# One block's diagonal, column sums and one-hot distances: three reorderings in a single-core kernel

## The reference, cut to what matters

```python
mod = c_act @ ada_w[l] + ada_b[l]
shift1, scale1, gate1, shift2, scale2, gate2 = jnp.split(mod, 6, axis=-1)
...                                            # pooling mixer and latent attention give y
x = x + gate1[:, None, :] * rms_norm(y, post_mix_g[l])
h = modulate(rms_norm(x, pre_ffn_g[l]), shift2, scale2)
y = peer_ffn(h, peer_wq[l], peer_sub_keys[l], peer_u[l], peer_v[l])
x = x + gate2[:, None, :] * rms_norm(y, post_ffn_g[l])
```

## Time and profile before

| what | value |
|---|---|
| median of 3 runs | 2076.1 us (2073.14 to 2076.58) |
| profiled execution, its own time | 2077.25 us |
| its span, first to last instruction | 2075.3 us |
| TensorE busy | 1905.2 us, 92% |
| VectorE busy | 1492.3 us, 72% |
| ScalarE busy | 948.2 us, 46% |
| POOL busy | 658.6 us, 32% |
| mean granted TensorE clock | 0.971 |

### The profile page before, as it was taken

The page is one execution under the profiler, slowest core; times in us unless marked ns, Lnnn a source line. Parts: engine busy times, 40 slices in busy tenths (PEclk is TensorE's granted clock), DMA queues, the critical chain, the costliest instruction groups (busy, mean ns, idle before and its releaser), DMA issues.

```text
span 2075.3 us, 33816 instructions
## 1 busy us (share of the span) xinstructions
PE 1905.2 (92%) x10307; PEld 1627.5 (78%) x10307; DVE 1492.3 (72%) x2053; ACT 948.2 (46%) x1498; POOL 658.6 (32%) x347
## 2 busy tenths in 40 slices
PE   0489989899999999999999997689999999999997
PEld 0479758799788888888888886578887888788886
DVE  6998679763888889998887668967675555455555
ACT  1043344443444444445554448854444444444443
POOL 1000020000888888889974446600000000000000
PEclk9789969899999999999999999999999999999999
DMA  9989569990666666666677762057766666665554
GB/s 390 415 306 384 201 254 385 287 219 19 164 187 186 185 187 185 185 187 175 184 191 189 189 159 91 0 184 286 288 233 183 203 204 207 234 210 194 192 193 151
DMA packets 229619, 439.10 MB, mean 212 GB/s; under 512 B 23538, under 2 KB 158144, under 8 KB 216000
## 3 DMA queue, kind: packets, MB, share of 16 engines
q1 hardware_dynamic: 225648, 416.31, 63.5%
q0 software_dynamic: 3888, 22.14, 3.0%
q10 hardware_dynamic: 32, 0.01, 0.0%
HBM read 434.12 MB, written 4.21 MB: 211 GB/s over the span
## 4 chain that ended last, share of the span: by engine, by line
PE 85%; DVE 6%; issue 4%; DMA 2%; ACT 1%; POOL 1%; SPq 1%; DVEq 0%; ACTq 0%; POOLq 0%
PE ps L883 21%; PE ps L885 11%; PE ps L933 11%; PE ps L934 11%; PE ps L936 11%; PE ps L655 4%; PE ps L657 4%; PE ps L656 4%; PE ps L916 3%; DVE acc L1338 3%; PE ps L650 2%; DMA raw<-in_peer_v_dram 1%; DMA i<-consts_dram 1%; POOL eL L546 1%; PE ps L644 1%
## 5 line engine op out<-in xcount | busy, mean ns | idle before, releaser
L883 PE MATMUL ps<-h,eH 128*128 128x512 f32 x2048 | 722.0, 397 | 5.7 <-POOL eL L546 5.6
L546 POOL TENSOR_TENSOR eL<-raw,eH 128x1024 fp32r<-128x1024 f32 x224 | 552.1, 2471 | 291.8 <-ACT eH L1192 291.6
L885 PE MATMUL ps<-h,eL 128*128 128x256 f32 x2048 | 574.8, 281 | 0.0
L1795 DVE TENSOR_TENSOR eL<-raw,eH 128x1024 fp32r<-128x1024 f32 x256 | 313.2, 1225 | 300.3 <-ACT eH L1285 300.2
L883 PEld LDWEIGHTS ps<-h,eH 128*128 128x128 f32 x2048 | 385.0, 188 | 100.3 <-POOL eL L546 8.0
L1285 ACT CAST eH<-raw 128x1024 fp32r<-128x1024 f32 x256 | 269.8, 1054 | 390.4 <-PE ps L936 336.5
L1192 ACT CAST eH<-raw 128x1024 fp32r<-128x1024 f32 x256 | 269.3, 1052 | 366.2 <-PE ps L885 303.0
L933 PE MATMUL ps<-eH,aH 128*128 128x512 f32 x1024 | 400.4, 391 | 7.3 <-DVE eL L1795 7.3
L934 PE MATMUL ps<-eL,aH 128*128 128x512 f32 x1024 | 400.0, 391 | 0.0
L1714 DVE STREAM_TRANSPOSE raw<-raw 128x1024 f32<-128x1024 f32 x256 | 317.2, 1242 | 104.7 <-DMA raw<-in_peer_u_dram 97.7
L885 PEld LDWEIGHTS ps<-h,eL 128*128 128x128 f32 x2048 | 387.4, 189 | 0.0
(11 more groups left out here) (270 smaller groups left out, 2360.0 us busy)
## 6 DMA issues: line engine op xcount, KB each, us to landing
raw<-in_peer_u_dram SPq DMA_DIRECT2D x1024, 128.0 KB, 2.9
raw<-in_peer_v_dram SPq DMA_DIRECT2D x256, 512.0 KB, 3.7
ring<-in_ada_w_dram SPq DMA_DIRECT2D x40, 2048.0 KB, 18.7
ring<-in_w_out_dram SPq DMA_DIRECT2D x8, 2048.0 KB, 16.1
ring<-in_peer_wq_dram SPq DMA_DIRECT2D x32, 512.0 KB, 19.4
piece<-in_ada_w_dram POOLq DMA_DIRECT2D x13, 1024.0 KB, 5.7
ring<-in_w_in_dram SPq DMA_DIRECT2D x6, 2048.0 KB, 14.9
ring<-in_w_uq_dram SPq DMA_DIRECT2D x2, 1536.0 KB, 9.0
```

Source lines behind the costliest of these rows:

```text
L546: pool.tensor_tensor(by_k(eL[:, j % RING, :]), turned(raw[:, j % RAW, :]), by_k(eH[:, j % RING, :].bitcast(F32)), ALU.subtract).then_inc(u ...
L883: pe.matmul(ps[:, bank, :], eH[:, slot, k * P:(k + 1) * P], h2[:, kk].rearrange("p a t -> p (a t)"), start=kk == 0, stop=False, skip_group ...
L885: mm = pe.matmul(ps[:, bank, 0:T], eL[:, slot, k * P:(k + 1) * P], h2H[:, kk, :], start=False, stop=kk == KT - 1, skip_group_check=True)
L1795: dve.tensor_tensor(eL[:, slot, :], raw[:, slot, :], eH[:, slot, :].bitcast(F32), ALU.subtract).then_inc(v_lo, 1)
```

## The change

It has three parts. On VectorE, the two columns of `mod2` are formed behind `diag` and no longer ahead of the wait for the squares; since they now read banks 0 and 1 while TensorE may transpose x1, these two banks come last in `X1_BANK`, and TensorE waits for `mod2_ready` ahead of block 12. Second, the low part of the second query weight is made behind the second pair of h2 and no longer behind the first. Third, ScalarE makes the distances of a group before the gated one-hots of the group ahead of it.

```diff
-X1_BANK = (2, 3, 0, 1, 4, 5, 6, 7)
+X1_BANK = (2, 3, 4, 5, 6, 7, 0, 1)
...
             pe.wait_ge(diag2, 2)
             for k in range(KT):
+                if k == 12:
+                    pe.wait_ge(mod2_ready, 2)
                 turn(lambda tt: x1q[:, tt, k * P:(k + 1) * P], X1_BANK[k // 2], k % 2, x1T_mm,
                      lambda tt: diag[:, tt, :])
...
-            def hot_first(g, q, first):
+            def distances(g, q, first):
                 if not first:
                     act.wait_ge(hot_mm, g - 3)
                 for t in range(2):
                     last_ = act.activation(hotA[:, q, t, :], iota, ACT.Abs,
                                            bias=slotT[:, 1, bass.ds(g * 4 + t, 1)], scale=-1.0)
                 last_.then_inc(hot_abs, 1)
+
+            def gated_hots(g, q):
                 act.wait_ge(hot_abs, g + 1)
                 for t in range(2):
                     last_ = act.activation(hotA[:, q, t, :], hotA[:, q, t, :], ACT.Relu,
...
             act.wait_ge(gate_minus, 1)
-            hot_first(0, 0, True)
+            distances(0, 0, True)
+            gated_hots(0, 0)
             gelu(TILES - 1, 1)
-            for q in range(1, 4):
-                hot_first(q, q, True)
+            distances(1, 1, True)
+            for q in range(2, 4):
+                distances(q, q, True)
+                gated_hots(q - 1, q - 1)
...
             with act.Fori(1, T // 16) as r:
                 for q in range(4):
-                    hot_first(r * 4 + q, q, False)
+                    distances(r * 4 + q, q, False)
+                    gated_hots(r * 4 + (q - 1), (q + 3) % 4)
+            gated_hots(T // 4 - 1, 3)
...
-            shift_column(mod2[:, 1, :], 3, 0, V_B3)
-            dve.nop().then_inc(mod2_ready, 1)
-            scale_column(mod2[:, 0, :], 4, 1, V_B4, V_G2)
-            dve.nop().then_inc(mod2_ready, 1)
             dve.wait_ge(x1_sq, 1)
...
                 seq(dve.tensor_scalar(diag[:, tt, :], ident, stat[:, 44 + tt:45 + tt], None, ALU.mult))
                 dve.nop().then_inc(diag2, 1)
+            shift_column(mod2[:, 1, :], 3, 0, V_B3)
+            dve.nop().then_inc(mod2_ready, 1)
+            scale_column(mod2[:, 0, :], 4, 1, V_B4, V_G2)
+            dve.nop().then_inc(mod2_ready, 1)
...
-                if j in (0, 2, 4, 6):
-                    weight_low("wq", 0, 1 + j // 2)
+                if j in (1, 2, 4, 6):
+                    weight_low("wq", 0, (0, 1, 2, 0, 3, 0, 4)[j])
```

## The result

The changed kernel takes 2058.5 us (median of 4 runs, 2054.4 to 2060.5) against 2076.3 us before: ratio 0.9913, 95% interval 0.9891 to 0.9935. The profiled execution took 2056.66 us with a span of 2054.8, against 2077.25 and 2075.3.

What follows compares the result with a forecast made beforehand. TensorE bounds the long stages; ScalarE, VectorE close behind, the scatter stage. 3.5 + 0 + 9.8 = 13.3 us, from 2077.25 to 2063.9, less 1.15 for the median: 2062.8; range 2059.0 to 2070.5 (own 2060 to 2066).

Steps and rivals of the forecast that it cites:

- The diagonal ahead of the columns: Around x1 at 400 us: transposes start when TensorE's column sums end, at about 404.05, 3.5 us sooner.
- rival B: Around x1: TensorE's instruction block is late and it stands until up to 407.7; 2066.3 us, chance 0.10.
- the whole block would move as it is: Around x1: transposes start at the low clock as before, 3.44 us long, so all 3.5 us stay.
- The clock's rise: At x1's transposes: a rise 1.7 us sooner or later would be worth some 0.8 us either way.
- The banks and the second low: Around x1: second h2 low 1.22 us sooner, but the projection waits for the transposes; worth 0, costs 0.
- Distances a round ahead: Scatter stage: ScalarE's 0.17 us wait goes, VectorE bounds at 2.92 us for two groups; 9.8 us gained in all.
- The end: End of the scatter stage: 63rd group's hotB to last gate multiply falls from 4.33 to 3.2 us, 1.1 gained.
- The start: Start of the scatter stage: the second gated pair stands behind one more distance pair; 0.4 us lost.
- Rivals A and C: Scatter stage: A, another bound near 3.1 us for two groups, 2068.0, chance 0.15; C, ScalarE's order gains nothing, 2073.0, 0.09.
- Rival D: Scatter stage: POOL becomes the bound, 3.64 us for two groups, 11.9 us longer there; 2084.5 us, chance 0.04.
- the runs' spread of 3.4 us: Whole kernel: spread of the three runs shown, counted in the forecast's own range of 2060 to 2066 us.

Runs made afterwards that it cites:

- after: The changed kernel with all three parts, in its first profile; median 2058.5 us, profiled execution 2056.66 us.
- before: The kernel without the change, in its first profile; 2076.3 us measured, profiled execution 2077.25 us.
- half-width hotP: Changed kernel with POOL's hotP written for 64 of its 128 columns and not read, TensorE reading hotD instead; 2062.1 us, ratio 0.9942.
- gates_half: Changed kernel with VectorE's multiply of the gates on only the first four of every eight tokens; 2054.7 us, ratio 0.9903.

## Why the prediction was right in its direction and 0.5 us out of its range

**The diagonal ahead of the columns: right.** Forecast were transposes right behind the column sums, 3.5 us sooner; measured 3.6 from the resumption, in all nine profiles with this edit, with the diagonal ready 0.8 us before it was wanted. No instruction stop came (rival B is out), and the wait before block 12 cost nothing. That the whole block would move as it is failed by 0.7 us: in after the distance from the resumption to the first u matmul fell from 122.95 us to 120.01, by 2.9 and not by 3.6. In the six profiles without the late stretch of the lower clock it fell by 3.5 to 3.7. The clock's rise, which I gave 0.8 us either way, took it. (To the 40th u matmul it is 132.4 against 129.2, the 3.3 of the sum above.)

**The banks and the second low: right**, 0. The second h2 low is 1.2 us sooner and the projection begins when the transposes end.

**Distances a round ahead: right mechanism, one term too small.** ScalarE's wait went, VectorE became the bound, and TensorE waits for hotD. The failed step is "the steady round without its wait (0.26, and some 0.08 of overlap lost with it) is 3.26 - 0.34 = 2.92". It left out that in the steady round of before one hotD takes 0.40 us, where an undisturbed one takes 0.33; 3.26 - 0.26 - 0.08 - 0.07 = 2.85, the fastest pair of the earlier trace rows, which I had set as the bound. The 0.40 stands in the rounds of before in which a hotP began 0.05 us ahead of the hotB (27 of the 28 long hotDs of that trace); in after no hotP of the steady rounds begins there. One begins under the multiply, the other 0.29 us inside a hotB, and though that one is held beside two hotDs, both take 0.33. Why the hotP that begins first lengthens hotD is not shown. So 29 x (3.233 - 2.851) = 11.1 us instead of 9.1. The end gave 1.3 (forecast 1.1). The start cost 0.4 as forecast: first hotB to 5th 8.6 us, before 8.2. That it fits so well is in part luck, since this distance is 7.6 to 8.4 us in the three profiles of the kernel before and 8.6 to 9.0 in those of the changed one. Sum 12.0, which the stage confirms: from the first scatter to the first product with v 107.8 - 95.9 = 11.9, and 11.1 to 11.2 in the two other profiles of the changed kernel. Rivals A and C are out: no bound at 3.1, and gated pairs follow the distances at full overlap.

**Rival D** did not come, yet my reason against it was wrong. I said that a hotP of 1.33 us "does proceed beside" hotB and hotD, since only 0.34 us were left behind them. The row fits being held off if the fixed 0.37 us can pass meanwhile, though not to the last digit: it ends 0.27 us after hotD and the half-width one 0.10, where their columns by the estimate need 0.42 and 0.21. The rule of the Trainium skill that I set aside (SBUF — State Buffer, SBUF: two separate sides) names VectorE operations in a 2-port mode, or with two SBUF inputs against a GpSimd operation that reads SBUF; hotB has two such inputs, and the multiply reads PSUM with one of its inputs. The trace agrees with it there (1.59 us for a half-width hotP under hotB and hotD, 0.58 beside the multiply); that hotD, with one SBUF tensor as input, runs in such a mode no run here shows. By the same rule whichever starts first gets the ports for its whole instruction. The trace does not agree with that: in the earlier trace rows hotP starts 0.06 us ahead of hotB, and hotP is the one that is held; a hotB of gates_half that starts 0.57 us before a hotP ends takes 0.76 us instead of 0.67. What failed was D's sum: it added POOL's whole 2 x 0.79 us to VectorE's time, while by the estimate only 2 x 0.42 need a free moment, and the multiply gives 1.13 in each round.

**The reference point: the larger part of the miss.** The edits together are worth 3.3 + 11.9 = 15.2 us by the profiles, 1.9 more than forecast. That alone, from the median shown, gives 2060.9, inside the range. The remaining 2.4 us are in the two medians. The second step that failed is "the runs' spread of 3.4 us" in the range, and with it the median of the same three runs, from which the sum is subtracted. I took the three runs of 2073.1 to 2076.6 us for what the kernel before takes and gave the runs a spread of 3.4 us; in 36 later runs, beside the experiments, it took 2066.4 to 2082.8 with a mean of 2074.1, and the changed kernel 2054.4 to 2065.8 with a mean of 2058.8 over its eleven. The means differ by 15.3 us, as the stages do. The profiled execution of before had both rates in it, and they could have been read there: 568 matmuls in the 100 us from 600, and in the later loop

```profile
1130.00:1200.00 70.00, 70.00 (x406) 1.00 0.75 190
```

which is 580 in 100 us, at the same full clock. A range that let each part come out either way would have been wider by 7 and 4 us.

## What to carry to other kernels

When one engine's wait is taken away and the next engine becomes the bound, price its round from its shortest records, step by step, and ask of each longer one whether its neighbour will still be there: the fastest rounds seen were the new steady state here, not the bound. Before an effect of some 0.3% is assigned to an edit, profile each kernel more than once and lay the traces side by side by instruction number, from stop to stop: a loop that no edit touches, with no idle and a full clock, can differ by 2% between executions. And when an engine is held off by another, do not add its whole instruction to the other's time: a hotP with 0.79 us of its own ended 0.25 to 0.27 us behind the hotD that held it.

## What the runs showed of the hardware that was not expected

- TensorE, never idle and at a granted clock of 1.00, ran the same alternating loop of 512 and 256 columns at 353.3 or at 346.7 ns a pair in every stretch between two stops, and changed from one to the other only at stops, also within a loop and between executions; two and two of them take 348.3 ns. The products with v, 512 columns throughout, take 226.7 ns a matmul in the steady part of every profile.
- POOL's tensor_scalar of 128 columns takes 0.79 us undisturbed, 0.58 at 64 columns; under VectorE's hotB and hotD it is held until they end, up to 1.77 us, also at half the width (1.79). Beside the multiply, which reads PSUM with one input, it takes its 0.79.
- VectorE loses little when POOL is first: a hotB that began 0.57 us before a hotP's end took 0.76 us instead of 0.67 (gates_half), one that began 0.31 us before it took 0.68 (before).
- The granted clock stood at the lower level for one stretch of 13.7 us around x1's transposes in all nine profiles with the first edit, but this stretch began anywhere from 3.8 to 5.4 us behind the first column sum, which was worth up to 0.7 us.
